# Even spacing of the split weight copies, and up groups of the MLP in products of 256 columns

## The reference

```python
mod = (c_act @ w_mod + b_mod)                     # six rows of 2048
h = rms_norm(x, norm1_g) * (1 + sc1) + sh1
z = h @ w_in                                      # attention, gates, convolution inputs
mixed = concat(fox(z), nsa(z), conv(z))
x = x + g1 * (mixed @ w_out)                      # 2048 x 2048
h = rms_norm(x, norm2_g) * (1 + sc2) + sh2
x = x + g2 * (square(relu(h @ w_mlp1)) @ w_mlp2)  # 2048 x 8192 and 8192 x 2048
return rms_norm(x, final_g)
```

## The kernel before, in words

| Tensor | before | after |
|---|---|---|
| near copies (w_hi, w_lo) | 160, 32, 32, 160 | 32, 32, 32, 32 |
| far copies (w_hi, w_lo) | 224, 224, 96, 96 | 96, 96, 96, 96 |
| act, u (hi and lo) | 160 | 32 |
| t copies (in mod_raw) | 224 | 96 |
| s copies 0, 1, 2 | 160, 32, 32 | 32, 32, 32 |

## Time and profile before

### The profile page before, as it was taken

How to read it: one execution, slowest core, us unless ns; L and a number is a source line. 1 busy time by engine, 2 the same in 40 slices (tenths; PEclk the granted TensorE clock), 3 DMA queues, 4 the chain that set the end, 5 groups by cost and what they waited for, 6 DMA issues and landing times.

```text
span 1165.0 us, 17842 instructions
## 1 busy us (share of the span) xinstructions
PE 1126.8 (97%) x7087; PEld 1000.1 (86%) x7087; DVE 983.4 (84%) x1182; ACT 642.1 (55%) x936; POOL 23.6 (2%) x40
## 2 busy tenths in 40 slices
PE   4999999999999999999999999999999999999996
PEld 4899989989887778999788888888888888888885
DVE  5998989988997988997887788987788987878775
ACT  6655448977775557545544445554445554445452
POOL 1000000100000000001000000000000000000000
PEclk7999999999999999999999999999999999999998
DMA  9999998878966898995566675657675657666451
GB/s 377 419 420 421 420 409 309 262 216 270 357 241 221 287 299 310 377 383 203 197 215 254 253 260 209 197 201 268 242 284 181 217 196 274 253 225 265 159 181 73
DMA packets 48323, 314.65 MB, mean 270 GB/s; under 512 B 6573, under 2 KB 8441, under 8 KB 11769
## 3 DMA queue, kind: packets, MB, share of 16 engines
q1 hardware_dynamic: 44592, 305.72, 70.5%
q0 software_dynamic: 1760, 5.26, 2.4%
q10 hardware_dynamic: 1896, 2.64, 0.8%
HBM read 305.20 MB, written 4.21 MB: 266 GB/s over the span
## 4 chain that ended last, share of the span: by engine, by line
PE 75%; DVE 12%; DMA 5%; ACT 5%; issue 4%; SPq 0%; ACTq 0%; DVEq 0%
PE quad L1314 15%; PE quad L1328 10%; PE quad L1330 9%; PE quad L1329 9%; PE quad L1316 8%; PE quad L1304 5%; PE quad L1305 4%; PE quad L1306 4%; DVE w_lo L1882 3%; DMA first_raw<-in_w_mod 3%; PE quad L1374 2%; PE quad L1376 2%; PE quad L1375 2%; DMA mod_raw<-in_w_mod 2%; DVE mod_raw L1889 2%
## 5 line engine op out<-in xcount | busy, mean ns | idle before, releaser
L921 ACT ACTIVATE w_hi<-raw 128x1024 fp32r<-128x1024 f32 (+1 forms) x342 | 355.6, 1045 | 296.8 <-PE quad L1330 113.0
L1882 DVE TENSOR_TENSOR w_lo<-raw,w_hi 128x1024 fp32r<-128x1024 f32 (+1 forms) x342 | 408.2, 1205 | 104.9 <-ACT w_hi L921 104.3
L1314 PE MATMUL quad<-act,w_hi 128*128 128x512 f32 x768 | 264.8, 390 | 0.0
L1304 PE MATMUL quad<-act,w_hi 128*128 128x256 f32 x760 | 214.5, 282 | 6.2 <-DVE w_lo L1882 4.1
L1316 PE MATMUL quad<-act,w_lo 128*128 128x256 f32 x768 | 213.7, 278 | 0.0
L1305 PE MATMUL quad<-act,w_hi 128*128 128x256 f32 x760 | 212.3, 279 | 0.0
L1306 PE MATMUL quad<-act,w_lo 128*128 128x256 f32 x760 | 212.2, 279 | 0.0
L1314 PEld LDWEIGHTS quad<-act,w_hi 128*128 128x128 f32 x768 | 144.6, 188 | 31.2
L1304 PEld LDWEIGHTS quad<-act,w_hi 128*128 128x128 f32 x760 | 144.4, 190 | 9.2 <-issue 6.3
L1328 PE MATMUL quad<-w_hi,u_hi 128*128 128x512 f32 x376 | 147.7, 393 | 0.8 <-DVE u_lo L2340 0.6
L1330 PE MATMUL quad<-w_hi,u_lo 128*128 128x512 f32 x376 | 147.4, 392 | 0.0
(11 more groups left out here) (371 smaller groups left out, 1718.5 us busy)
## 6 DMA issues: line engine op xcount, KB each, us to landing
raw<-in_w_main SPq DMA_DIRECT2D x184, 1024.0 KB, 5.0
mod_raw<-in_w_mod SPq DMA_DIRECT2D x67, 1024.0 KB, 7.6
first_raw<-in_w_mod SPq DMA_DIRECT2D x14, 1024.0 KB, 15.7
late_raw<-in_w_mod SPq DMA_DIRECT2D x10, 1024.0 KB, 8.2
acc<-in_w_mod SPq DMA_DIRECT2D x4, 1024.0 KB, 12.4
conv_b<-conv_q POOLq DMA_DIRECT2D x8, 512.0 KB, 5.5
x_a<-in_x SPq DMA_DIRECT2D x2, 1024.0 KB, 6.9
x_scratch<-x SPq DMA_DIRECT2D x1, 2048.0 KB, 12.3
```

Source lines behind the costliest of these rows:

```text
L921: A(dst[:, 0:2 * width], block_half(raw, j, width), ACT.Copy).then_inc(hi_done, 1)
L1304: mm(out, hi, act_hi[:, k, :], start=begin and m % 2 == 0, stop=False, skip_group_check=True)
L1314: mm(out, w_hi[MERGED[0]][j % 4][:, cols], act_both[:, k, :, :].rearrange("p h t -> p (h t)"), start=begin, stop=False, skip_group_check=True)
L1882: TTn(lo[:, 0:2 * width], block_half(raw, j, width), hi[:, 0:2 * width].bitcast(f32), ALU.subtract)\
```

## The change

The slots become 4352 bytes wide, a multiple of 256, and BEAT becomes 256, so the remainders are those of the right column of the table above: every slot stands alike to the activations modulo 256. The up groups of quarters two to four use `feature_rows` with both weight copies far, into one pair of banks per group (pair 0, 1, 2, 3 in turn). ScalarE takes the relu from PSUM, VectorE only squares. The loop over the up groups on TensorE is written out, and its waits name the pair's earlier user.

```diff
-BEAT = 128
+BEAT = 256
-        w_hi_slot = [sb(f"w_hi{i}", [P, 2 * GW + SHIFT], f32r) for i in range(4)]
-        w_lo_slot = [sb(f"w_lo{i}", [P, 2 * GW + SHIFT], f32r) for i in range(4)]
+        w_hi_slot = [sb(f"w_hi{i}", [P, 2 * GW + BEAT // 4], f32r) for i in range(4)]
+        w_lo_slot = [sb(f"w_lo{i}", [P, 2 * GW + BEAT // 4], f32r) for i in range(4)]
         def views(slots, far):
-            return [slots[i][:, (i + far) % 2 * SHIFT:(i + far) % 2 * SHIFT + 2 * GW] for i in range(4)]
+            return [slot[:, far * SHIFT:far * SHIFT + 2 * GW] for slot in slots]
...
-            def copy_rest(q, i):
+            def relu_up(q, i):
                 act.wait_ge(u_ready, q * 4 + i)
-                banks = quad[i % 2][:, :].rearrange("p (m h t) -> p m h t", m=4, h=2)
-                A(relu[:, :].rearrange("p (k t) -> p k t", k=4), banks[:, :, 1, :], ACT.Copy).then_inc(up_copy, 1)
+                A(relu[:, :], pair[i][:, :], ACT.Relu).then_inc(up_used, 1)
...
-                            weight_hi(g, j, kind=MERGED if i < 4 else BY_TOKEN)
+                            weight_hi(g, j, kind=BY_FEATURE if i < 4 else BY_TOKEN)
...
-                        last = merged_rows(par, j, k, kk, k == 0, k == KT - 1)
+                        last = feature_rows(par, j, k, kk, k == 0, k == KT - 1)
...
             def mlp_up(q):
-                with pe.Fori(0, 2) as i:
-                    for par in range(2):
-                        pe.wait_ge(evac_dve, q * 4 + (3 + par))
-                        pe.wait_ge(up_used, q * 4 + i * 2 + (par - 1))
-                        up_group(q * 8 + i * 2 + (G_MLP + par), par)
+                for i in range(4):
+                    if i % 2 == 0:
+                        pe.wait_ge(evac_dve, q * 4 + (3 + i // 2))
+                    up_group(q * 8 + G_MLP + i, i)
...
-                        pe.wait_ge(up_used, q * 4 + (3 + cg))
+                        pe.wait_ge(up_used, q * 4 + 2 * cg + 2)
...
-            def up_sum(q, i):
-                banks = quad[i % 2][:, :].rearrange("p (m h t) -> p m h t", m=4, h=2)
-                dve.wait_ge(up_copy, q * 4 + (i - 3))
-                r3 = relu[:, :].rearrange("p (k t) -> p k t", k=4)
-                TTn(r3, r3, banks[:, :, 0, :], ALU.add).then_inc(up_used, 1)
+            def square_up(q, i):
                 dve.wait_ge(up_used, q * 4 + (i + 1))
-                STT(relu[:, :], relu[:, :], 0.0, relu[:, :], ALU.max, ALU.mult).then_inc(up_square, 1)
+                TTn(relu[:, :], relu[:, :], relu[:, :], ALU.mult).then_inc(up_square, 1)
```

More of the change, by code:

```diff
@@ L84 @@
 NEAR, FAR = 0, 1
-BY_TOKEN, BY_FEATURE, MERGED = (NEAR, NEAR), (FAR, FAR), (FAR, NEAR)
+BY_TOKEN, BY_FEATURE = (NEAR, NEAR), (FAR, FAR)
 def kind_in(n):
@@ L555, in build @@
         up_square = sem("up_square")
-        up_copy = sem("up_copy")
         u_cast = sem("u_cast")
@@ L1246, in mlp_quarter @@
                             act.wait_ge(pe_half, g * 8)
-                            copy_rest(q, i - 1)
+                            relu_up(q, i - 1)
                         if j == 6 and 1 <= i <= 4:
@@ L1307, in feature_rows @@
                 return last
[L1309 to L1318, removed]
             def token_rows(par, j, k, kk, a_hi, a_lo, begin, end, width=GW, tiles=range(TT), weights=None):
@@ L1855, in _ @@
             for cg in range(3):
-                pe.wait_ge(up_used, (QUARTERS - 1) * 4 + (3 + cg // 2))
+                pe.wait_ge(up_used, (QUARTERS - 1) * 4 + cg + 1)
                 if cg == 2:
@@ L2496, in mlp_quarter @@
                         if j == 5 and 1 <= i <= 4:
-                            up_sum(q, i - 1)
+                            square_up(q, i - 1)
                         if j == 6 and 1 <= i <= N_SPLIT and not final:
@@ L2515, in mlp_quarter @@
                         else:
-                            weight_lo(q * 8 + (G_MLP + i), j, kind=MERGED if i < 4 else BY_TOKEN)
+                            weight_lo(q * 8 + (G_MLP + i), j, kind=BY_FEATURE if i < 4 else BY_TOKEN)
                         if (i, j) in GATE_AT[:GATE_ROWS[q]]:
```

## The result

| | Before | After |
|---|---|---|
| Median | 1164.20 us (7 runs, 1162.92 to 1165.43) | 1169.43 us (7 runs, 1168.43 to 1172.70) |
| Profiled execution, span | 1166.99, 1165.0 us | 1169.06, 1167.1 us |
| VectorE, ScalarE busy | 983.4, 642.1 us | 970.0, 641.0 us |

The ratio is 1.0043, with a 95% interval of 1.0029 to 1.0056: 5.2 us slower where 3.9 were forecast (1168.2 us).

What follows compares the result with a forecast made beforehand. In the MLP TensorE never idles, so the pace of its products was taken as the bound. +6.7 - 3.3 - 0.7 + 0.8 + 0.4 = +3.9 us on the 1164.27 us median gave 1168.2 us; 8-in-10 range 1156 to 1171.5 us.

Steps and rivals of the forecast that it cites:

- Slow pace in the up groups: Up groups of quarters two to four: the new 256-column products run at 117.8 ns, +2.24 us a quarter, +6.7 us in all.
- Down groups in step: MLP down groups: with distance 0 in every slot, 42 slow halves fall by 0.08 us each, taken as -3.3 us.
- Combined halves: Combined halves of 10 groups: second and third also go to 2.47 us like the first, +0.8 us (0.6 to 1.2).
- Output projection: Output projection: 16 slow halves gain 0.08 us each, half of it counted for attention steps between, -0.7 us (0 to -1.3).
- first quarter: First quarter's up groups: a disturbed stretch after 527.67 us would stay slow longer, +0.4 us (0 to 3.4).
- VectorE and ScalarE: Up groups: 12 additions go, 14.6 us of VectorE; relu replaces a like-shaped copy; TensorE waits for neither, 0 us.
- (a): Rival: the up groups lock to the fast pace, 113.3 ns; -6.8 us, 1157.5 us; chance 0.33.
- (b): Rival: spacing does nothing, the pattern by slot has another cause; -3.6 us, 1160.7 us; chance 0.07.
- (c): Rival: the address itself counts, 32 being slow; down groups' slots 0 and 3 fall to 233 ns; +13 us, 1177 us; chance 0.05.

## Why the prediction was right

**Slow pace in the up groups, +6.7 us.** Right, mechanism and size: 90.46 us for each quarter against a forecast of 90.47, three times +2.23. That the entry decides is shown by one extra product turning 90.46 into 87.11 us; that a change of slot class can free the stream is shown at 642.39 us in the kernel with the old slots. One leg of the reasoning is weaker than it looked: the fast first quarter was held to be fast because it is entered after transposes and waits. With the old slots and the new products it has the same entry and the same addresses as before, and its first 144 products take 17.05 us, 118.4 ns each, before it turns to 113.3. So that entry leaves either pace open.

**Down groups in step, -3.3 us.** Right in its reason, mis-sized. The distance decides, as the two moves by 128 bytes show, and all plain halves now take 2.72 us. But 20 of the 42 slow halves stand directly behind a combined half, and I priced them like the others. The one from 725.64 to 728.43 us took 2.79 us before; after the change it takes 2.76, since its first products still run slow after the combined half, at any slot. So those 20 gained 0.03 and not 0.08 us each, 1 us less. Those rows before, which I had not read apart:

```profile
725.64 0.40 PE L1328 MATMUL quad<-w_hi,u_hi 128*128 128x512 f32 x1
...
728.43 0.28 PE L1374 MATMUL quad<-w_hi,u_hi 128*128 128x256 f32 x1
```

**Combined halves, +0.8 us.** Right: all at 2.47 to 2.48 us. Down groups and combined halves together were forecast at -2.5 us and came to -1.2 in the traces, which is the 1.3 us by which 3.9 fell short of 5.2.

**Output projection, -0.7, first quarter, +0.4.** The first quarter's 624 products took 70.8 us after and 71.1 before: a disturbance at 527.67 us did not come again, so the +0.4 was not needed. That was in part luck, as the slow pace of the same stretch with the slots 128 bytes off (73.57 us) shows what could have come. The -0.7 has the right direction: three unbroken pieces of the output projection, 108 of its 384 products, took 25.38 us before (from 294.69, 301.86 and 421.05 us) and 25.03 after. The rest of the term is open: the start of the first quarter's stretch scatters between 470.2 and 471.6 us over six kernels with even spacing, the far distance of 64 bytes and the input projection unchanged, against 471.9 and 473.3 us in the two with the old spacing.

**VectorE and ScalarE, 0.** Right: VectorE lost 13.4 us of work and TensorE waited 1.0 us for it in the MLP, as good as before.

**Rivals.** (a) is what one extra product makes of the kernel; its 1157.5 us stands against 1159.5 measured. (b) fell with the slots 128 bytes off, at 1178.5 us, and with the far distances of 64 and 128 bytes, which differ by 14.1 us (1159.6 against 1173.7 us). The rule of the Trainium skill ("TensorE: Matmul & The Clock Gate", "Step-by-step: what each phase is for"), that loading the next weights takes nothing from the running product, would let all distances run alike, and these runs do not bear it out. (c) fell with all addresses moved by 128. What a lock is in the hardware is not settled: the runs show which distances and entries give which pace, not why.

## What to carry to other kernels

Where TensorE has no idle time, read the pace from start to start, half by half, and look for a pattern by buffer: equal work at two paces, with no wait in the trace, was an address effect here, and mending it alone gave 5.5 us for 192 bytes more per slot. Before changing the width of a product, look up in the trace how its new width runs in the place from which it will be entered, not only where it runs best. Two changes that are good apart may take from each other what made them good: here uneven slots were what shook the 256-column stream loose.

## What the runs showed of the hardware

Paces in the kernels with even spacing, behind the first products of a stretch; the last column is the mean over the 21 products of a combined half:

| Start of the weights less that of the activations, modulo 256 | 512 columns, weights moving, ns | 256 columns, weights loaded, ns | 256 columns, weights moving, ns |
|---|---|---|---|
| 0 | 226.7 | 120.0 | 119.6 |
| 32 | not run | 118.3 | 116.8 |
| 64 | not run | 113.3 or 117.8 | 118.0 |
| 128 | 233 | 118.7 | 119.8 |
| 192 | not run | 117.8 | 117.8 |

All are 4-byte operands on this one core, the activations starting 32 bytes past a multiple of 64. With the weights loaded 64 bytes above the activations both paces hold for hundreds of products (768 in 90.46 or in 87.12 us), and in quarters two to four the same entry gives the same pace each time. At 192 bytes the fast pace was seen only where slots at 64 and at 192 take turns (the old slots, 672 products at 113.3 ns) and for eight products at the start of some combined halves with the slots 128 bytes off; 768 and 624 products at 192 alone all ran slow. That one product of 128 columns decides the pace of the 768 behind it was the surprise, and so was that the same trick fails in the combined halves, where the moving operand lies above the loaded one.
